# The hand-overs inside the recurrent mixers of a three-block transformer: copy order on ScalarE, six remainders moved from GpSimd to VectorE, own weight tiles for one output piece

## The reference

```
proj = hn @ w_mix_in[l]
p_att, p_rwkv, p_conv = split(proj)
y_att  = sliding_window_sink_attention(p_att, ...)     # 512 wide
y_rwkv = rwkv7_time_mix(p_rwkv, ...)                   # 256 wide, a recurrence over the tokens
y_conv = short_conv_mix(p_conv, conv_w[l])             # 256 wide: b_gate * conv(c_gate * h)
mixed  = concatenate([y_att, y_rwkv, y_conv]) @ w_mix_out[l]
h = h + (1 + gt2) * mixed
```

## Time and profile before

| | |
|---|---|
| median of 3 runs | 2921.03 us (2919.41 to 2924.48) |
| the profiled execution, own time | 2915.46 us |
| its span in the trace | 2913.7 us |
| mean granted TensorE clock | 0.966 |
| TensorE, VectorE, ScalarE, GpSimd busy | 95%, 51%, 33%, 7% |
| share of TensorE in the chain that ended last | 89% |

### The profile page before, as it was taken

One profiled execution on the slowest core, in us unless ns is written; L12 is line 12 of the kernel. 1 busy time (PEld: TensorE's weight loads), 2 busy tenths in 40 slices (PEclk: granted clock), 3 DMA queues, 4 the chain that ended last, 5 costly groups with the idle time before them and its releaser, 6 DMA issues.

```text
span 2913.7 us, 42233 instructions
## 1 busy us (share of the span) xinstructions
PE 2755.8 (95%) x17756; PEld 2246.5 (77%) x17756; DVE 1490.7 (51%) x1826; ACT 966.6 (33%) x1464; POOL 200.5 (7%) x271
## 2 busy tenths in 40 slices
PE   6999999898999999999999889999999999968996
PEld 5888877687888878888777778888777777558775
DVE  6565666745565443333457543333355557655533
ACT  3222234523222232222345223222324445232322
POOL 3000000410000000000002300000000000022000
PEclk9999999989999999999999889999999999879998
DMA  7565542103565222232221012232321221100231
GB/s 285 196 228 202 187 152 76 44 17 110 200 211 214 83 98 101 79 115 79 88 87 62 3 58 101 84 109 81 109 94 58 80 73 66 47 2 3 76 108 44
DMA packets 45513, 299.68 MB, mean 103 GB/s; under 512 B 5552, under 2 KB 5680, under 8 KB 16944
## 3 DMA queue, kind: packets, MB, share of 16 engines
q1 hardware_dynamic: 36144, 230.35, 22.8%
q0 software_dynamic: 9216, 67.11, 6.3%
HBM read 295.35 MB, written 2.10 MB: 102 GB/s over the span
## 4 chain that ended last, share of the span: by engine, by line
PE 89%; DVE 7%; ACT 2%; DMA 1%; issue 1%; POOL 0%; SPq 0%; DVEq 0%; ACTq 0%; POOLq 0%
PE ps L917 17%; PE ps L918 17%; PE ps L919 17%; PE ps L1205 6%; PE ps L1206 5%; PE ps L1207 5%; PE ps L1512 2%; PE ps L1513 2%; PE ps L1514 2%; PE ps L2041 1%; PE ps L2025 1%; PE ps L2038 1%; DMA ada_first<-in_ada 1%; DVE w_lo L894 1%; PE ps L1327 1%
## 5 line engine op out<-in xcount | busy, mean ns | idle before, releaser
L917 PE MATMUL ps<-hn_hi,w_hi 128*128 128x512 f32 x1536 | 603.1, 393 | 36.1 <-DVE hn_lo L867 17.0
L918 PE MATMUL ps<-hn_lo,w_hi 128*128 128x512 f32 x1536 | 601.7, 392 | 0.0
L919 PE MATMUL ps<-hn_hi,w_lo 128*128 128x512 f32 x1536 | 601.2, 391 | 0.0
L894 DVE TENSOR_TENSOR w_lo<-w_raw,w_hi 128x2048 fp32r<-128x2048 f32 (+3 forms) x229 | 472.4, 2063 | 180.6 <-ACT w_hi L887 177.1
L887 ACT ACTIVATE w_hi<-w_raw 128x2048 fp32r<-128x2048 f32 (+3 forms) x229 | 394.5, 1723 | 115.8 <-PE ps L1207 97.4
L917 PEld LDWEIGHTS ps<-hn_hi,w_hi 128*128 128x128 f32 x1536 | 291.1, 190 | 100.1 <-issue 39.4
L919 PEld LDWEIGHTS ps<-hn_hi,w_lo 128*128 128x128 f32 x1536 | 290.8, 189 | 61.1
L918 PEld LDWEIGHTS ps<-hn_lo,w_hi 128*128 128x128 f32 x1536 | 291.1, 189 | 60.2
L1205 PE MATMUL ps<-hn_hi,w_hi 128*128 128x512 f32 x776 | 323.6, 417 | 7.7 <-DVE hn_lo L867 4.9
L1206 PE MATMUL ps<-hn_lo,w_hi 128*128 128x512 f32 x776 | 306.5, 395 | 0.0
L1207 PE MATMUL ps<-hn_hi,w_lo 128*128 128x512 f32 x776 | 306.0, 394 | 0.0
(11 more groups left out here) (449 smaller groups left out, 3384.9 us busy)
## 6 DMA issues: line engine op xcount, KB each, us to landing
w_raw<-in_up SPq DMA_DIRECT2D x88, 1024.0 KB, 4.8
ada_w<-in_ada POOLq DMA_DIRECT2D x64, 1024.0 KB, 5.1
w_raw<-in_down SPq DMA_DIRECT2D x64, 704.0 KB, 4.0
w_raw<-in_mix_in SPq DMA_DIRECT2D x20, 1024.0 KB, 4.8
w_raw<-in_dsa_in SPq DMA_DIRECT2D x18, 1024.0 KB, 4.8
w_raw<-in_merge SPq DMA_DIRECT2D x16, 768.0 KB, 4.2
ada_first<-in_ada SPq DMA_DIRECT2D x8, 1024.0 KB, 12.6
w_raw<-in_mix_out SPq DMA_DIRECT2D x8, 1024.0 KB, 4.8
```

Source lines behind the costliest of these rows:

```text
L894: dve.tensor_tensor(w_lo[:, slot, 0:size], w_raw[:, slot, 0:size], w_hi[:, slot, 0:size].bitcast(F32), ALU.subtract).then_inc(w_lo_ready, 1)
L917: pe.matmul(bank, wh, x_hi[:, k], start=(k == 0), stop=False)
L918: pe.matmul(bank, wh, x_lo[:, k], start=False, stop=False)
L919: return pe.matmul(bank, wl, x_hi[:, k], start=False, stop=(k == K - 1))
```

## The change

Four edits, in both layers' mixers.

1. ScalarE copies `rw_bt` before it rounds the attention's and the convolution's output. TensorE's wait for `rw_kt` moves from ahead of the recurrence to ahead of the first reading of the state.
2. GpSimd writes the convolution's product to `conv_out` (tiles 10 and 11 of `proj`, after VectorE has read them) and makes no remainders.
3. VectorE makes the remainders, a tile at a time: one after each of levels 0 to 3 of the first group, two after level 4. It waits for the convolution's product instead of the first remainder.
4. The third output piece gets weight tiles of its own, `third_hi` and `third_lo`. ScalarE rounds it right after the second piece, VectorE makes its remainder between `reciprocal` and the normalisation.

```
-                pool.tensor_tensor(conv_y, conv_y, proj[:, 18:20], ALU.mult).then_inc(conv_ready, 1)
-                pool.wait_ge(conv_hi, l + 1)
-                pool.tensor_tensor(hn_lo[:, 6:8], conv_y, hn_hi[:, 6:8].bitcast(F32), ALU.subtract).then_inc(others_lo, 1)
-                pool.wait_ge(att_out_hi, l + 1)
-                pool.tensor_tensor(hn_lo[:, 0:4], proj[:, 0:4], hn_hi[:, 0:4].bitcast(F32), ALU.subtract).then_inc(others_lo, 1)
+                pool.wait_ge(factors_ready, 2 * v)
+                pool.tensor_tensor(conv_out, conv_y, proj[:, 18:20], ALU.mult).then_inc(conv_ready, 1)
...
             pe.wait_ge(rw_tokens_a, v)
-            pe.wait_ge(rw_tokens_b, v)
             rw_delta_pe(pe, rwu[l])
...
-            pe.wait_ge(others_lo, 2 * v)
+            pe.wait_ge(others_lo, len(OTHERS) * v)
...
             def out_piece(i, odd):
+                if i == 2:
+                    pe.wait_ge(w_lo_ready, p1 + 3)
+                    pe.wait_ge(act_evac, p1 + 1)
+                    pe.wait_ge(dve_evac, p1 + 1)
...
+                            wh, wl = third_hi[:, col:col + P], third_lo[:, col:col + P]
+                            pe.matmul(bank, wh, hn_hi[:, k], start=(k == 0), stop=False)
...
+        def others_low(dve, l, n):
+            k = OTHERS[n]
+            dve.wait_ge(att_out_hi if k < 4 else conv_hi, l + 1)
+            src = proj[:, k] if k < 4 else conv_out[:, k - 6]
+            dve.tensor_tensor(hn_lo[:, k], src, hn_hi[:, k].bitcast(F32), ALU.subtract).then_inc(others_lo, 1)
...
                 level_x_pe(pe, d, 0, m)
+            pe.wait_ge(rw_tokens_b, d.phase + 1)
             read_pe(pe, d, 0, 0)
...
                 level_dve(dve, d, 0, m)
+                if m < LEVELS - 1:
+                    others_low(dve, d.phase, m)
+            others_low(dve, d.phase, 4)
+            others_low(dve, d.phase, 5)
             rhs_dve(dve, own, d, 0, 0)
...
+            act.wait_ge(rw_turned, 3 * l + 2)
+            act.activation(rw_bt[:].rearrange("p a b c -> p a (b c)"), ps[:, 2:4], ACT.Copy).then_inc(rw_tokens_a, 1)
             act.wait_ge(piece_done, p_end)
             act.wait_ge(att_out, 8 * v)
             act.activation(hn_hi[:, 0:4], proj[:, 0:4], ACT.Copy).then_inc(att_out_hi, 1)
             act.wait_ge(conv_ready, v)
-            act.activation(hn_hi[:, 6:8], conv_y, ACT.Copy).then_inc(conv_hi, 1)
-            act.wait_ge(rw_turned, 3 * l + 2)
-            act.activation(rw_bt[:].rearrange("p a b c -> p a (b c)"), ps[:, 2:4], ACT.Copy).then_inc(rw_tokens_a, 1)
+            act.activation(hn_hi[:, 6:8], conv_out, ACT.Copy).then_inc(conv_hi, 1)
...
             split_act(act, (p1 + 1, (p1 + 1) % 2), WIDE)
+            act.wait_ge(raw_loaded[p1 % 2], 8 * (p1 + 2) + (16 if p1 % 2 == 0 else 8))
+            act.activation(third_hi[:], w_raw[:, p1 % 2], ACT.Copy).then_inc(w_hi_ready, 1)
...
-                if i == 0:
-                    split_act(act, (p1 + 2, p1 % 2), WIDE)
...
-            dve.wait_ge(others_lo, 2 * l + 1)
+            dve.wait_ge(conv_ready, v)
             rw_delta_dve(dve, own, rwu[l])
...
             dve.reciprocal(head_roots[:], head_roots[:]).then_inc(gn_rooted, 1)
+            dve.wait_ge(w_hi_ready, p1 + 3)
+            dve.tensor_tensor(third_lo[:], w_raw[:, p1 % 2], third_hi[:].bitcast(F32), ALU.subtract).then_inc(w_lo_ready, 1)
```

More of the change, by code:

```diff
@@ L241, in program @@
         d_u = tiles("d_u", 42, 1, [P, 2, 2, HD])
+        conv_out = proj[:, 10:12]
+        third_hi = tiles("third_hi", 4, 4, [P, WIDE], dt=F32R)
+        third_lo = tiles("third_lo", 15, 4, [P, WIDE], dt=F32R)
         ds_q = [tiles(f"ds_q{g}", 4 * g, 4) for g in range(3)]
@@ L1944, in out_piece @@
             def out_piece(i, odd):
+                if i == 2:
+                    pe.wait_ge(w_lo_ready, p1 + 3)
+                    pe.wait_ge(act_evac, p1 + 1)
+                    pe.wait_ge(dve_evac, p1 + 1)
+                    for t in range(2):
+                        bank = main[p1 % 2][t]
+                        for k in range(KD):
+                            col = (2 * k + t) * P
+                            wh, wl = third_hi[:, col:col + P], third_lo[:, col:col + P]
+                            pe.matmul(bank, wh, hn_hi[:, k], start=(k == 0), stop=False)
+                            pe.matmul(bank, wh, hn_lo[:, k], start=False, stop=False)
+                            last = pe.matmul(bank, wl, hn_hi[:, k], start=False, stop=(k == KD - 1))
+                    last.then_inc(piece_done, 1)
+                    return
                 pe_piece(pe, p1 + i, (p1 + odd) % 2, KD, 2, hn_hi, hn_lo, lambda k: None)
@@ L2519, in out_piece @@
                 s = (p1 + odd) % 2
-                if i == 0:
-                    split_act(act, (p1 + 2, p1 % 2), WIDE)
-                elif i > 1:
+                if i > 1:
                     split_act(act, *ahead(p1, KD // 2, WIDE, i, odd))
@@ L2680, in out_piece @@
                 s = (p1 + odd) % 2
-                if i == 0:
-                    split_dve(dve, (p1 + 2, p1 % 2), WIDE)
-                elif i != 1:
+                if i > 1:
                     split_dve(dve, *ahead(p1, KD // 2, WIDE, i, odd))
```

## The result

The change made the kernel faster, by 0.7%. In the runs taken together with the kernel before, its median is 2899.88 us (2895.05 to 2902.39, 4 runs) against 2921.91 (2919.41 to 2924.48, 4 runs): a ratio of 0.9929, 95% interval [0.9906, 0.9952], so 14 to 27 us. The same kernel, measured once more beside others later, gave 2902.01 and a ratio of 0.994 [0.9918, 0.9962]. Forecast were 2902.4 us, 18.6 less than before. The profiled execution took 2898.23 us.

The account below looks back on a forecast made before the run. TensorE, busy 95% of the span, bounds the kernel, so only its waits and low clock can yield time. A and B 10.3, C 1.5, E 7.6, D -0.8: 18.6 us off 2921.03 gives 2902.4, range 2894 to 2912.

Parts of the forecast that it names:

- Term A: Hand-over to the first matrices: with `rw_bt` copied earlier, the masks start 2.38 us sooner per layer.
- Term B: First group's masks: without long GpSimd instructions beside them, 4.86 us instead of 7.64 to level 0's second half, 2.78 gained.
- Term C: Level 0: shorter idle times keep TensorE's clock up in one of two layers, 1.5 us gained for both together.
- Term D: Remainders on VectorE: four hide between levels, the two behind level 4 delay the second group; 0.4 us lost per layer.
- Term E: Output stage: no wait ahead of the third piece, 3.09 us per layer, plus 1.4 of half clock in layer 1; 7.6 together.
- the masks stayed at 0.68: Rival, chance 0.09: L2077 meets another GpSimd instruction or the levels wait for GpSimd, so the masks stay long; 2909.5 us.
- the normalisation kept 0.71 of slack: Rival, chance 0.08: the third piece's remainder starts late and delays the normalisation; about 2906 us.
- the remainders stayed off the path: Rival, chance 0.04: each remainder on VectorE waits for a GpSimd copy and no gap covers it; 2923 us, no change.
- Half clock through the levels: Rival, chance 0.03: VectorE's extra work thins TensorE's stream and levels 1 to 4 run at half clock; 2929 us, slower.

Follow-up runs that it names:

- copy_last: The changed kernel, but ScalarE copies `rw_bt` last again, behind both roundings; ratio 0.9945 to the kernel before.
- gpsimd_remainders: The changed kernel, but GpSimd makes the two remainders again, behind its convolution product; ratio 0.9972 to the kernel before.
- warm: The changed kernel plus three matmuls per layer with unused results, in the idle times around level 0's first half; ratio 0.9928 to the kernel before.
- third_only: The kernel before with only the third output piece's own weight tiles and earlier split added; ratio 0.9985 to the kernel before.
- again: The changed kernel, nothing altered, measured once more later; 2902.01 us, ratio 0.994 to the kernel before.
- no_third: The changed kernel with the third output piece split as before, all other edits kept; ratio 0.9962 to the kernel before.
- gpsimd_late: The changed kernel, but GpSimd makes the remainders behind its level copies for the first group, and VectorE none; ratio 0.995 to the kernel before.

## Why the prediction was right, point by point

*Term A, the hand-over:* forecast 2.38 per layer, measured 2.41 and 2.42. What comes next was named rightly as well: GpSimd's product releases the masks. `copy_last` shows that the new product can't take over unless the copy has moved.

*Term B, the masks:* forecast 2.78, measured 2.79 and 2.78. The step that gives the whole loss to the long L2077 was only part of it. The lock-out is real (`gpsimd_remainders`), and in the kernel before it held up the second half of level 0 by 1.0 to 1.4 us, by the estimate above. The rest is that GpSimd's copies stood behind its remainders, which the sum left out. The second group's 4.86 us, from which the term was sized, was free of both, so the number held whatever the shares were; that it did not need them was luck.

*Term C, the clock of level 0:* forecast a gain of 1.5 us for both layers together, measured a loss of 1.4. This is the step that failed, and in both layers. "With the change the idle times there shrink" was true (2.27 and 1.14), and the clock fell all the same. It fell earlier and came back in the window of 581, so that it covered 2.3 and 2.05 us' worth of path instead of 1.4. `warm` shows that it is the clock: filled idle time gives 14.03 us. The size of the loss is less sure than its cause, for it rests on one trace of each kernel. `third_only` has the old order there and takes 24.34 and 23.21 us from the masks to level 4, beside 23.07 and 23.14 before; the changed kernel takes 21.15 and 20.93, and 20.92 and 21.22 in `again`. On these means the gain of B and C together is 2.4 us per layer where 2.78 + 0.75 was forecast. I had reckoned that shorter idle times keep the clock up in one layer of two; they did so in neither, nor in `again`.

*Term D, the remainders on VectorE:* forecast 0.4 lost per layer, measured 0.47 and 0.21 behind level 4; between the levels they hide. The price of meeting GpSimd showed up on GpSimd (1.78 instead of 1.42), off the path.

*Term E, the third piece:* forecast 7.6, measured 2.91 + 5.81 = 8.7. The waits of 3.09 are gone in both layers. In layer 1 there is more. The third piece itself, from its start to the mixer's end, took 25.41 us in layer 1 and takes 23.92, 1.5 less where 1.4 had been counted. The rest is a half-clock stretch that I had not priced. Before, the low clock of layer 1's chunk stage went on behind the start of the centring (1678.53); the windows of the kernel before:

```profile
1679.00:1680.00 1.00, 1.00 (x3) 0.71 (x3) 1.00 (x2) 0.21 (x1) 0.00 (x0) 0.50 0.00 0
1680.00:1681.00 1.00, 1.00 (x5) 0.82 (x4) 1.00 (x1) 0.85 (x1) 0.00 (x0) 0.68 0.00 0
```

Up to about 1680.6 that is 2.1 us at half speed, 1.0 lost. In the changed kernel the centring starts at 1667.59 and the clock is back at about 1667.04, just ahead of it:

```profile
1667.00:1668.00 1.00, 1.00 (x5) 0.68 (x4) 0.41 (x1) 1.00 (x2) 0.00 (x0) 0.98 0.00 0
```

3.09 + 1.5 + 1.0 = 5.6 of the 5.81. In layer 0 it is the other way round: the clock was back at 643 before, just ahead of the centring, and is back at about 639.6 now, 0.8 us behind its start (638.81): 3.09 - 0.4 = 2.7 of the 2.91. `no_third` had neither of layer 1's two half-clock losses and still had the wait, so the 1.4 us that the prediction counted for the clock was right for this trace of the kernel before, but is no lasting property of the wait.

*The recorded readings.* They hold but for one: by its window (0.67) the chunk stage's half clock began at about 629.3, not 629.7, which changes nothing in the sum.

*Sum:* 18.6 forecast; 17.7 in the mixers' stages, 17.2 in the span, 22.0 in medians and 17.4 in the second comparison. C was 2.9 too high and E 1.1 too low; these misses partly cancel against each other and against +0.7 in the chunks, which I did not follow up. 2902.4 was right within what the runs resolve, and the closeness of the total owes something to luck.

*The rivals:* L2077 met GpSimd's first copy, the masks stayed at 0.68; the normalisation kept 0.71 of slack; the remainders stayed off the path. Half clock through the levels did not come, but a part of it did: the clock stayed low up to the window of 581.

## What to carry to other kernels

When a long instruction on one engine lengthens one on another, look at both queues: what stands behind the long one may cost as much as what is locked out, and a wait ahead of a single copy (0.96 us here) tells which of the two set that step. Cutting the long instruction into pieces shortened the mask and filled the queue, and gave nothing here; moving it to after the urgent work, on its own engine or another, cured both. A gap in front of small matmuls can be paid for twice, as waiting and as half clock behind it. Matmuls that are needed anyway, placed in such gaps of the last four chunks, kept the clock at full there and were done on the side. What one trace says of the clock is one sample: look at a second one before you price it. Read small edits by the stage they touch: 2 us per layer were plain there and invisible in the ratio.

## What the runs showed of the hardware that was not expected

The clock fell with shorter idle times than before: after its 64x64 matrices TensorE waited 2.27 us and then ran 16 small matmuls, and the granted clock was already down to 0.89 in the window of 574. In the kernel before, an idle time of 3.21 us behind 128x128 matmuls had left it at full. Whether the size of the matmuls makes the difference is not shown. The moment of the fall also moves with nothing changed in the work: in `again` the clock is at 0.65 in the window of 573, so it fell at about 573.3, while TensorE still waited (the matmuls start at 573.55), and in `gpsimd_late`, with the same wait of 2.28 us, it holds 1.00 until the window of 576 (0.70).

In the chunk stage TensorE counts as fully busy in the window of 626, with 20 matmuls, and gets 0.50; with guests of 128x512 between the steps the window of the same name gets 1.00 at the same busy time. The busy time of a window did not tell which clock it was granted.

Six remainders of one tile took 7.9 us on GpSimd where two instructions for the same elements took 6.9. Not all of it is the price of cutting: uncut, the second one took 4.95 us instead of 4.51 where it met a long mask at its start (`gpsimd_remainders`), and the pieces meet two masks that took 1.50 and 1.51.
